# One hybrid decoder layer on one Trainium2 core: the second block of each norm tile is rotated, scaled and stored later, and the second map's score maximum is taken before the norm

## What is computed

```python
h = rmsnorm(x, norm_w)
proj = h @ w_in                        # 2048 x 6400
qa, ka, va, ga, qb, kb, vb, gb = split(proj)
qa = apply_rope(rmsnorm(qa per 64 columns, q_norm_a), cos, sin)     # ka, qb, kb likewise
# A: 8 heads, causal, 128-query blocks, two softmax maps per head
a  = softmax(q0 @ k0.T / 8) - lam * softmax(q1 @ k1.T / 8)
ya = rmsnorm(a @ va, subln_w) * (1 - lam_init) * silu(ga)
# B: 16 query heads on 2 kv heads, window of 128, sinks
yb = softmax_with_sink(qb @ kb.T / 8) @ vb * silu(gb)
out = x + concat(ya, yb) @ w_out       # 2048 x 2048
```

## Time and profile before

| what | value |
|---|---|
| median of 3 runs (lowest, highest) | 1862.24 us (1861.84, 1863.05) |
| the profiled execution's own time | 1863.16 us |
| its span, first to last instruction | 1861.4 us |
| granted TensorE clock, mean | 0.991 of full speed |
| DVE busy | 1099.3 us, 59% |
| ACT busy | 798.1 us, 43% |
| POOL busy | 397.6 us, 21% |

### The profile page before, as it was taken

How to read it: one execution, slowest core, us unless ns; L and a number is a source line. 1 busy time by engine, 2 the same in 40 slices (tenths; PEclk the granted TensorE clock), 3 DMA queues, 4 the chain that set the end, 5 groups by cost and what they waited for, 6 DMA issues and landing times.

```text
span 1861.4 us, 27812 instructions
## 1 busy us (share of the span) xinstructions
PE 1804.5 (97%) x8920; PEld 1504.7 (81%) x8920; DVE 1099.3 (59%) x2247; ACT 798.1 (43%) x2116; POOL 397.6 (21%) x640
## 2 busy tenths in 40 slices
PE   5999999999999999999999999999999799999999
PEld 4788888788888888888888888888888678788887
DVE  7633565765657656576565766758667866333333
ACT  7311445454454544544445444544444544222221
POOL 1211221312213122141221412314133521000000
PEclk8999999999999999999999999999999899999999
DMA  6222222222222222222222222323334544444445
GB/s 230 61 72 79 79 79 67 73 88 74 79 71 72 83 75 81 72 72 83 71 85 73 73 85 82 97 84 83 111 83 124 172 121 127 160 162 151 143 143 175
DMA packets 254583, 186.00 MB, mean 100 GB/s; under 512 B 29088, under 2 KB 225696, under 8 KB 253344
## 3 DMA queue, kind: packets, MB, share of 16 engines
q1 hardware_dynamic: 254496, 184.90, 32.6%
HBM read 139.75 MB, written 45.09 MB: 99 GB/s over the span
## 4 chain that ended last, share of the span: by engine, by line
PE 80%; DVE 10%; issue 3%; ACT 3%; DMA 3%; POOL 1%; SPq 1%; DVEq 0%; ACTq 0%
PE ps_a L836 20%; PE ps_a L838 19%; PE ps_a L837 19%; PE ps_b L920 3%; PE ps_b L836 3%; PE ps_b L837 3%; PE ps_b L838 3%; PE ps_a L880 2%; DVE stage_rows L1101 2%; PE ps_a L879 2%; PE ps_b L935 2%; PE ps_b L873 2%; DVE hT_lo L1101 2%; DMA qkv_sb<-qkv_a_dram 1%; PE ps_b L966 1%
## 5 line engine op out<-in xcount | busy, mean ns | idle before, releaser
L836 PE MATMUL ps_a<-hT_hi,w_hi_sb 128*128 128x512 f32 x1696 | 694.9, 410 | 8.0 <-DVE stage_rows L1182 4.5
L838 PE MATMUL ps_a<-hT_hi,w_lo_sb 128*128 128x512 f32 x1696 | 666.7, 393 | 0.0
L837 PE MATMUL ps_a<-hT_lo,w_hi_sb 128*128 128x512 f32 x1696 | 664.1, 392 | 0.0
L1101 DVE TENSOR_TENSOR w_lo_sb<-w_raw_sb,w_hi_sb 128x512 fp32r<-128x512 f32 (+1 forms) x320 | 227.0, 712 | 273.8 <-ACT w_hi_sb L641 271.7
L836 PEld LDWEIGHTS ps_a<-hT_hi,w_hi_sb 128*128 128x128 f32 x1696 | 321.4, 190 | 71.6 <-issue 7.3
L838 PEld LDWEIGHTS ps_a<-hT_hi,w_lo_sb 128*128 128x128 f32 x1696 | 320.2, 189 | 71.8
L837 PEld LDWEIGHTS ps_a<-hT_lo,w_hi_sb 128*128 128x128 f32 x1696 | 321.9, 190 | 58.0
L641 ACT ACTIVATE w_hi_sb<-w_raw_sb 128x512 fp32r<-128x512 f32 (+1 forms) x320 | 197.8, 621 | 231.2 <-DMA w_raw_sb<-in_w_out 96.2
L799 ACT ACTIVATE expd<-ps_a,neg_max 128x256 f32<-128x256 f32 (+7 forms) x128 | 95.1, 743 | 212.9 <-DVE neg_max L1239 210.6
L731 ACT ACTIVATE attention_parts<-ps_b 128x512 fp32r<-128x512 f32 (+3 forms) x160 | 76.9, 521 | 222.3 <-PE ps_b L920 222.1
L1101 DVE TENSOR_TENSOR ps_a<-ps_a,mask 128x128 f32<-128x128 f32 (+2 forms) x192 | 77.5, 417 | 140.3 <-PE ps_a L880 138.8
(11 more groups left out here) (128 smaller groups left out, 2594.7 us busy)
## 6 DMA issues: line engine op xcount, KB each, us to landing
w_raw_sb<-in_w_in SPq DMA_DIRECT2D x200, 256.0 KB, 3.0
w_raw_sb<-in_w_out SPq DMA_DIRECT2D x104, 256.0 KB, 3.1
qkv_a_dram<-stage_rows SPq DMA_DIRECT2D x48, 256.0 KB, 2.4
qkv_sb<-qkv_a_dram SPq DMA_DIRECT2D x64, 192.0 KB, 2.9
gates_dram<-stage_rows SPq DMA_DIRECT2D x32, 256.0 KB, 2.7
gate_y<-gates_dram SPq DMA_DIRECT2D x128, 64.0 KB, 2.5
y_dram<-gate_y SPq DMA_DIRECT2D x128, 64.0 KB, 2.4
x_raw_sb<-in_x SPq DMA_DIRECT2D x6, 1024.0 KB, 6.3
```

Source lines behind the costliest of these rows:

```text
L836: pe.matmul(dst, a_hi, b_hi, start=start, stop=False)
L837: pe.matmul(dst, a_hi, b_lo, start=False, stop=False)
L838: return pe.matmul(dst, a_lo, b_hi, start=False, stop=stop)
L1101: return dve.tensor_tensor(o, a, b, op)
```

## The change

The second block (b = 1) of each norm tile, turned in half step 5 or 9, is rotated by DVE and scaled by POOL one half step later (6 or 10), behind `lo_probs`, and stored by SP two half steps later (7 or 11). The first block stays where it was. For mixer A the second map's maximum (`max_a(cur, 1)`) goes ahead of `rows_out` in every odd half step; only in 5, 9 and 13 is there a `rows_out` to pass. ACT's evacuation no longer waits for POOL's scaling of the tile before (`rst_ready`) but for the release of its transposes (`tp_free`), except for the first kv tile. The number of compute instructions and DMAs is the same. The diff:

```diff
--- before.py
+++ after.py
@@ -347,6 +347,11 @@
 
             return OK // 4 * P if proj_kind(first + 1 + s // 16) == "O" and s // 16 < 2 else 512
 
+        def norm_block_back(it, first, s, back):
+
+            tb = turned_before(it, first, s - back) if s >= back else None
+            return tb if tb and tb[0]["norm"] and tb[2] == 1 else None
+
         def turned_before(it, first, s):
 
             d, u, before = proj_tile(it, first, s)
@@ -578,7 +583,10 @@
                     elif back2 and back2["k"] == "A":
                         store_y(back2, it, first)
                     tb = turned_before(it, first, s)
-                    if tb:
+                    late = norm_block_back(it, first, s, 2)
+                    if late:
+                        store_rows(late[0], 1, None)
+                    if tb and not norm_block_back(it, first, s, 0):
                         store_rows(tb[0], tb[2], use_number(tb[1], it, first))
                     if d and d["kind"] == "O" and s % 4 == 2:
                         for b in range(2):
@@ -672,7 +680,7 @@
 
                 if before is None:
                     return
-                if before["norm"]:
+                if before is KV_TILES[0]:
                     wait(act, rst_ready[b], before["K"] + 1)
                 elif before["turned"]:
                     n = (use_number(("PT", before["p"], b), it, first) if before is not KV_TILES[1]
@@ -1362,6 +1370,9 @@
                     if s % 2 and cur and cur["k"] == "B":
                         sum_b(cur)
                     tb = turned_before(it, first, s)
+                    late = norm_block_back(it, first, s, 1)
+                    if s % 2 and cur and cur["k"] == "A":
+                        max_a(cur, 1)
                     if tb:
                         n = use_number(tb[1], it, first)
                         rows_out(tb[0], tb[2], n, bank_of(tb[1], first))
@@ -1373,8 +1384,6 @@
                         if back1:
                             lo_probs(back1, it, first)
                     else:
-                        if cur and cur["k"] == "A":
-                            max_a(cur, 1)
                         if back1 and back1["k"] == "A":
 
                             wait(dve, sm["o_second"], back1["G"] + 1)
@@ -1384,8 +1393,10 @@
                         nk = cur["k"] if cur and i + 1 < NR else kind(first + 1) if i + 1 == NR else None
                         if nk:
                             lo_qk(nk, (i + 1) % NR, it, first)
-                    if tb:
+                    if tb and not norm_block_back(it, first, s, 0):
                         rotate(tb[0], tb[2], n)
+                    if late:
+                        rotate(late[0], 1, use_number(late[1], it, first))
 
             iterations(dve, body)
 
@@ -1516,8 +1527,11 @@
                                 .then_inc(sm["o_pow"], 1)
                         if cur:
                             lo_v(cur)
-                    if tb:
+                    late = norm_block_back(it, first, s, 1)
+                    if tb and not norm_block_back(it, first, s, 0):
                         scale_rows(tb[0], tb[2])
+                    if late:
+                        scale_rows(late[0], 1)
 
             iterations(pool, body)
 
```

## The result

| | before | change |
|---|---|---|
| median, us | 1862.85 | 1841.18 |
| ratio of medians, 95% interval | | 0.9882 [0.9867, 0.9897] |
| profiled execution, its span, us | 1863.16, 1861.4 | 1839.11, 1837.3 |

The median fell by 21.7 us; the forecast had 19.0 (1843.2 us, range 1840.5 to 1850.0). A later series of the same changed kernel gave 1840.34. One of the five executions took 2002.04 us at a much lower granted clock and is not used.

The account below looks back on a forecast made before the run. PE was taken as the bound, with 19.0 us of stops in the A iterations: load 7.8, `turn_o` 6.7, the rest 4.5. From the median, 1862.24 - 19.0 = 1843.2 us; range 1840.5 to 1850.0.

Parts of the forecast that it names:

- The bound: PE is busy 97% of the span; its stops in the A iterations can give back at most 19.0 us.
- Store, 7.8 us: Storing two half steps later ends all 8 `turn_qk` waits for the q, k, v rows' load: 7.8 us off.
- Rotation, 6.7 us: Rotating behind `lo_probs` ends the 8 waits of `turn_o` at half step 11: 6.7 us off.
- Maximum, 4.5 us: Maximum ahead of `rows_out` ends the `scores_a` waits behind half steps 5 and 9; with scattered stops, 4.5 us off.
- What the rotation hits: The moved rotation delays DVE in half steps 7 and 11: mixer A nothing, mixer B 0 to 0.3 us per iteration, taken as 0.
- the forecast's other bound: The moved rotation takes 2.46 us instead of 2.19 beside POOL, making the B term 0.8 us.
- Rival 1: The scores' waits stay because the maximum's move only swaps one wait for another: 1847.7 us, 7%.
- Rival 2: POOL's scaling gets ahead of the low part at half steps 7 and 11, giving back 4.3 us: 1847.5 us, 8%.
- Rival 3: Only the load's wait goes; the rotation ahead of half steps 7 and 11 makes equally long new waits: 1854.4 us, 6%.
- Rival 4: Slower: DVE has no room in half steps 7 and 11, so PE waits at 8 and 12: 1895.8 us, 2%.
- Rival 5: Nothing changes, because the store did not hold the load nor DVE the turns: 1862.2 us, 2%.
- contention term: The moved rotation could lose 0.27 us beside POOL in each of 3 B iterations: 0.8 us, not in the forecast sum.

Follow-up runs that it names:

- e1: The kernel before with only the store of each norm tile's second block moved two half steps later; 1854.21 us, ratio 0.9953.
- e2: The kernel before with only mixer A's second-map maximum moved ahead of `rows_out`; 1841.32 us, ratio 0.9881.
- e7: The change with five extra 128-column multiplies on DVE ahead of each late rotation; 1843.02 us, ratio 0.9891.
- e4: The change with the late rotation ahead of `lo_probs` instead of behind it; 1849.98 us, ratio 0.9931.
- e6: The change with the first part of y loaded in half step 12 and split in half step 14 instead of 15; 1836.43 us, ratio 0.9855.

## Why the prediction was right, and where it was not

*The bound.* PE alone, by its idle time in the A iterations: right. The 19.0 us were 2.7 us short of the 21.71. Set matmul against matmul by their starts in both traces, the kernel before has 31 stops with an idle time above 0.02 us, the number that was an estimate: 9 at `turn_qk` cost 8.4 us, 8 at `turn_o` 7.1 and 14 at `scores_a` 5.9, 21.4 us in all. Each costs its idle time plus 0.16 us, as I had it, and something on the matmul behind it, which I left out: 0.1 us behind the scores' stops (1.5 us), 0.03 to 0.06 behind the others (0.9 us). The last 0.3 us lie in no stop. Taking starts in place of idle time was the right choice: idle time alone is 14.0.

*Store, 7.8 us.* Right as a step taken by itself: 8.3 in e1. *Rotation, 6.7 us.* On top of the store, 951.34 - 944.22 = 7.1 us: right in size. *Maximum, 4.5 us.* On top of both, 6.3 us: mis-sized.

*The attribution failed.* The step "all 8 waits go" of the store and "5.4 + 8 x 0.16 = 6.7 us go" of the rotation gave each wait to one edit. e2 shows that one late instruction fed all three waits and that the maximum alone gives 20.4 of 21.7 us; in another order of adding the parts, the store is worth 1.7 us and the rotation nothing. My text had the number in hand: it worked out that `lo_qk` ends 1.4 us earlier, and that DVE is at half step 10 "1.4 us earlier", but did not hold this against the waits of 0.5 to 1.0 us that it explained otherwise. The total came out right because it was never built from the parts: it was PE's whole idle time by starts, with the third part as what was left (19.0 - 14.5), so the overlap could not be counted twice. The rotation was not run alone, and what it gives by itself is not known. I also took the load's 2.9 us from the earlier trace rows, a median; in this iteration it took 3.3 us, and PE resumed as it landed.

*One cause, not memory.* The 22 waits repeat once per iteration at the same half steps. The Trainium skill ("Perfetto Trace Analysis", Optimization Strategy) says that such consistent bubbles can mean that SBUF or PSUM is too small for the next tile. `turn_o`'s wait for a bank looks like that. Here it was another cause: with the same buffers and only the mask and the maximum moved, e2 has none of these bank waits.

*What the rotation hits.* It takes 340.54 - 338.35 = 2.19 us in its new place, as forecast; the low part behind it 0.68 us. In mixer B the low part of half step 11 was forecast 0.07 us later; it starts at 1285.75, which is 1308.17 less the shift of 1399.52 - 1377.09 = 22.43 us, to 0.01. Cost nothing: right, but with nothing to spare (e7), so any loss of DVE beside POOL there (0.27 us in the forecast's other bound) would have been paid in full in each of the three iterations.

*The rivals.* None came. Rival 1: the scores' waits are gone. Rival 2: POOL's scaling did not hold the low part (0.68 us), because it started 0.16 us behind it, at 340.70; the scaling was the one that lost time, and nothing waited for it. Where the scaling starts first, the low part takes 1.29 us (e4, last section), so the hold is real and the order decides. My remark that the low part's 0.68 us beside the scaling spoke against contention was a misreading: it showed only that the low part went first. Rival 3: DVE's lateness did not move on. Rival 4 has a true core in mixer B alone: the 1.01 us of delay on DVE was exposed in full there (e7), while mixer A took the same delay for nothing. Rival 5 fell with the first run.

## What to carry over

When an engine's waits repeat in one pattern under different names (a load, a bank, an operand), write each one's time from a common start and ask whether they are late by the same amount: in-order lists hand one late instruction's delay on unchanged, and one reordering at its head can do what three do at its ends. Price parts as steps in a stated order, and test the cheapest one alone. Count stops by starts, the matmul behind the stop included, and before calling a moved block free, measure how much more would still be free.

## What the runs showed of the hardware

In some pairings DVE and POOL hold each other up, and the one that starts first wins. The low part of the weights on DVE and the scaling on POOL both take their inputs from SBUF. In the change the low part starts at 340.54 and takes 0.68 us, and the scaling comes second:

```profile
340.70 1.42 POOL L1475 TENSOR_TENSOR stage_rows<-stage_rows,ss_h 128x512 f32<-128x512 f32 x1 [4.60 <-DVE stage_rows L1109]
```

In e4_rot_first, at the same half step, the scaling comes first:

```profile
342.37 1.04 POOL L1475 TENSOR_TENSOR stage_rows<-stage_rows,ss_h 128x512 f32<-128x512 f32 x1 [4.13 <-DVE stage_rows L1109]
```

```profile
342.20 0.55 DVE L1109 TENSOR_TENSOR attention_parts<-ps_b,attention_parts 128x384 fp32r<-128x384 f32 x1
342.67 1.29 DVE L1109 TENSOR_TENSOR w_lo_sb<-w_raw_sb,w_hi_sb 128x512 fp32r<-128x512 f32 x1
```

These are the same two instructions. The scaling takes 1.42 us when it comes second and 1.04 when it comes first; the low part takes 0.68 us first and 1.29 second. In the change all 50 scalings start 0.16 us behind a low part and take 1.42 us; in e4 28 do, and the 22 others take 1.04. `lo_probs`, which still runs on DVE when the scaling of e4 starts and reads one of its inputs from PSUM, does not hold it. The Trainium skill ("SBUF — State Buffer", Terms, shared port pair) says that the pair is exclusive, held for the full instruction, and that the loser fully blocks. The trace agrees for this pairing; a POOL instruction on 8 columns did not block so: the low part that starts at 1133.62 in the change takes 0.68 us, 0.24 us into one of 1.64 us.

The same is seen where y is split on both engines. The second run of the change, the weights' low part of 384 columns alone and then behind two of y's splits, and POOL's own splits:

```profile
1417.42 0.55 DVE L1109 TENSOR_TENSOR w_lo_sb<-w_raw_sb,w_hi_sb 128x384 fp32r<-128x384 f32 x1
...
1428.04 3.11 DVE L1109 TENSOR_TENSOR hT_lo<-hT_lo,hT_hi 128x512 fp32r<-128x512 f32 x2 [0.26 <-ACT hT_hi L775]
1431.07 1.61 DVE L1109 TENSOR_TENSOR w_lo_sb<-w_raw_sb,w_hi_sb 128x384 fp32r<-128x384 f32 x1
```

```profile
1427.13 5.14 POOL L1495 TENSOR_TENSOR hT_lo<-hT_lo,hT_hi 128x512 fp32r<-128x512 f32 x3 [10.29 <-ACT hT_hi L775]
```

The low part takes 1.61 us instead of 0.55, and the two splits 3.11 us, where three take 1.89 us with POOL idle (e6, from 1426.26). How much the second one loses depends on what is left of the first. e4's low part found 0.74 us of the scaling left and lost 0.61 us; the scaling of the change found 0.52 us left and lost 0.38; the cosine multiply of the earlier trace rows found 0.42 us left of a POOL instruction that takes 0.46 us (from 340.41) and lost 0.27; the low part of 384 columns found 1.20 us left and lost 1.06. So the 0.27 us of the forecast's contention term are no fixed price.
